# Hymba/MoE layer on one core: the last couple of experts gets a pass of its own order

## What is computed

```python
h = rms_norm(x, norm_ffn_g[l])
# top-1 group of 4, top-2 experts of its 8; combine[token, expert] holds the weights
a = jnp.einsum('sd,edf->sef', hs, w_gate)          # 32 experts, 1024 -> 256
u = jnp.einsum('sd,edf->sef', hs, w_up)
act = jax.nn.silu(a) * u * cs[..., None]
x = x + jnp.einsum('sef,efd->sd', act, w_down)     # 256 -> 1024
return rms_norm(x, norm_final_g)
```

## Time and profile before

| | us |
|---|---|
| median of 3 runs | 355.81 |
| the three runs | 355.76, 355.81, 357.69 |
| the profiled execution | 356.66 |
| its span | 354.8 |
| PE busy | 314.8 |
| DVE, ACT, POOL busy | 167.0, 121.1, 46.2 |
| mean DMA rate over the span | 341 GB/s |

### The profile page before, as it was taken

One profiled execution on the slowest core, in us unless ns is written; L12 is line 12 of the kernel. 1 busy time (PEld: TensorE's weight loads), 2 busy tenths in 40 slices (PEclk: granted clock), 3 DMA queues, 4 the chain that ended last, 5 costly groups with the idle time before them and its releaser, 6 DMA issues.

```text
span 354.8 us, 11527 instructions
## 1 busy us (share of the span) xinstructions
PE 314.8 (89%) x4766; PEld 244.4 (69%) x4767; DVE 167.0 (47%) x461; ACT 121.1 (34%) x308; POOL 46.2 (13%) x79
## 2 busy tenths in 40 slices
PE   8999999999999999979799899999999758649482
PEld 5999899799775446666577677777777555526460
DVE  4759285554164513844355355555555514322233
ACT  3544254463244237423233133333333302121113
POOL 3400001642504037600000000000000000000001
PEclk9999999999999999999999999999999989998878
DMA  7999994081849998699999999999999999999933
GB/s 270 321 388 386 386 396 171 14 342 21 336 136 388 307 400 328 235 294 411 421 404 385 413 421 409 417 421 414 422 417 414 413 413 426 414 416 420 415 127 118
DMA packets 33669, 121.07 MB, mean 341 GB/s; under 512 B 5624, under 2 KB 8080, under 8 KB 26480
## 3 DMA queue, kind: packets, MB, share of 16 engines
q1 hardware_dynamic: 33312, 120.63, 87.0%
q10 hardware_dynamic: 336, 0.14, 0.1%
HBM read 119.72 MB, written 1.05 MB: 340 GB/s over the span
## 4 chain that ended last, share of the span: by engine, by line
PE 69%; SPq 15%; DMA 6%; issue 3%; ACT 3%; DVE 2%; POOLq 0%; POOL 0%; ACTq 0%; DVEq 0%
PE bank L547 13%; PE bank L807 13%; SPq L389 8%; PE bank L614 7%; PE bank L839 6%; DMA spare<-in_w_up_dram 6%; PE bank L761 6%; PE bank L541 5%; SPq L401 5%; PE bank L768 3%; SPq L383 2%; PE bank L561 2%; PE bank L576 1%; PE bank L828 1%; PE bank L523 1%
## 5 line engine op out<-in xcount | busy, mean ns | idle before, releaser
L807 PE MATMUL bank<-ring,hT 128*32 128x128 f32 x1664 | 54.1, 283 | 18.7 <-DMA ring<-in_w_up_dram 8.7
L807 PEld LDWEIGHTS bank<-ring,hT 128*32 128x32 f32 x1664 | 47.7, 114 | 27.6 <-issue 27.4
L1546 DVE SCALAR_TENSOR_TENSOR yb<-bank,pp,yb 64x512 fp32r<-64x512 f32 x34 | 25.5, 750 | 50.8 <-ACT yb L1080 50.3
L1263 DVE TENSOR_TENSOR unit_lo<-ring,unit_hi 128x2048 fp32r<-128x2048 f32 (+1 forms) x12 | 26.5, 2209 | 28.7 <-ACT unit_hi L909 28.7
L1080 ACT ACTIVATE yb<-bank,pp 64x512 fp32r<-64x512 f32 x34 | 23.2, 683 | 35.4 <-PE bank L839 35.0
L761 PEld LDWEIGHTS bank<-pp,qk 128*128 128x128 bf16 x912 | 29.1, 100 | 8.1 <-issue 5.6
L761 PE MATMUL bank<-pp,qk 128*128 128x64 bf16 x912 | 31.4, 196 | 2.8 <-issue 2.8
L614 PE MATMUL bank<-ring,qk 128*128 128x512 f32 (+1 forms) x72 | 29.9, 551 | 0.0
L1225 POOL TENSOR_SCALAR stats<-qk 128x1 f32<-128x1 f32 x2 | 0.6, 311 | 200.5 <-ACT work L1100 200.5
L807 PE MATMUL bank<-work,hT 128*32 128x128 f32 x320 | 21.4, 288 | 5.4 <-DMA spare<-in_w_up_dram 2.9
L1529 DVE SCALAR_TENSOR_TENSOR pp<-bank,stats,pp 128x128 f32<-128x128 f32 x18 | 6.3, 351 | 41.5 <-ACT pp L1069 41.5
(11 more groups left out here) (217 smaller groups left out, 527.4 us busy)
## 6 DMA issues: line engine op xcount, KB each, us to landing
ring<-in_w_up_dram SPq DMA_DIRECT2D x24, 1024.0 KB, 16.7
ring<-in_w_down_dram SPq DMA_DIRECT2D x24, 1024.0 KB, 17.4
ring<-in_w_gate_dram SPq DMA_DIRECT2D x16, 1024.0 KB, 15.9
ring<-in_w_in_dram SPq DMA_DIRECT2D x5, 2048.0 KB, 19.7
ring<-in_w_gate_dram SPq DMA_DIRECT2D x16, 512.0 KB, 13.8
ring<-in_w_out_dram SPq DMA_DIRECT2D x4, 1024.0 KB, 12.8
spare<-in_w_gate_dram SPq DMA_DIRECT2D x4, 1024.0 KB, 18.7
spare<-in_w_up_dram SPq DMA_DIRECT2D x4, 1024.0 KB, 19.1
```

The lines of the kernel that those rows point to most:

```text
L807: last = mm(p_gu[b:b + CAP, w * P:(w + 1) * P], hg[:, k, CAP * e:CAP * (e + 1)], w_gu[at[e]][:, w, k, h, :], start=(k == 0), stop=(k == KD ...
L1263: V.tensor_tensor(unit_lo[b][:, k, :], unit_src(u)[:, k, :], unit_hi[b][:, k, :].bitcast(fp32), ALU.subtract).then_inc(w_lo_ready, 1)
L1546: V.scalar_tensor_tensor(out=yb[half][rest, :], in0=p_y[rows, :], scalar=wcol[rows, :], in1=yb[half][rows, :].bitcast(fp32), op0=ALU.mult, ...
```

## The change

- PE's loop runs 3 rounds instead of 4. The fourth round is written out behind it: `one_pass` for couples 12, 13 and 14 and a new `last_pass` for couple 15.
- `last_pass` has the same work in another order: the sums of the pass before first; four products that nobody reads; gates; picks; gather and the turned selection; three unread products; ups; three unread products; the activation turned round; then the downs in two halves, with the final norm's weights spread by two products of the PE ahead of each half.
- The downs of the places of couples 3, 7, 11 and 15 come in four transfers of 512 KB (first halves of both experts, then second halves), with a second semaphore. At the couples' first loading each expert's two halves are issued one after the other.
- The 512 KB transfer of the final norm's weights goes. One of 4 KB (`gfin4`, four rows) is issued ahead of the first refill. ACT and DVE copy the spread halves from the banks into `gfin`.

```diff
+            sp.dma_start(gfin4, I["norm_final_g"].rearrange("(r c) -> r c", r=4)).then_inc(gfin_in, 16)
             for q in range(TURN):
                 refill(q, [(2 * (q + TURN) + i, places(q)[i]) for i in range(2)])
             ...
-            sp.wait_ge(gate_done, sp.value_load(base[0:1, COUPLES - TURN + 1:COUPLES - TURN + 2], min_val=1, max_val=ITEMS_MAX))
-            sp.dma_start(gfin, I["norm_final_g"].rearrange("(o d) -> o d", o=1).to_broadcast([P, D])).then_inc(gfin_in, 16)
```

```diff
+            def load_dn_part(e, p, f):
+                src = I["w_down"][0, bass.ds(e, 1), f * P:(f + 1) * P].rearrange("o p n -> p (o n)")
+                sp.dma_start(w_dn[p][:, f], src).then_inc((dn_in, dn2_in)[f][p], 16)
...
-                for e, p in loads:
-                    load_dn(e, p)
+                if loads[0][1] in places(TURN - 1):
+                    for f in range(2):
+                        for e, p in loads:
+                            load_dn_part(e, p, f)
```

```diff
+            def last_pass(i, q, at, fillings, edge):
+                def unread_into(dst, n):
+                    for _ in range(n):
+                        mm(dst[:, :], identb, cb[:, 0:HALF], start=True, stop=True)
+                def spread_gfin(half, dst):
+                    for r in range(2):
+                        row = 2 * half + r
+                        mm(dst[:, r * SEQ:(r + 1) * SEQ], ident[0:4, row:row + 1].to_broadcast([4, P]), gfin4, start=True, stop=True)
+                pe.wait_ge(selT_ready, i + 1)
+                add_result(i)
+                unread_into(p_y, 4)
+                pe.wait_ge(hg_half_ready, i + 1)
...
+                    last = gate_or_up(0, k, at)
...
+                pe.wait_ge(sel_ready, i + 2)
+                gather(p_hg).then_inc(gathered, 1)
...
+                unread_into(p_y, 3)
+                for e in range(2):
+                    pe.wait_ge(up_in[at[e]], fillings * 16)
+                for k in range(KD):
+                    last = gate_or_up(1, k, at)
+                last.then_inc(gu_done, 1)
+                unread_into(p_y, 3)
+                pe.wait_ge(act_ready, i + 1)
+                nc.tensor.transpose(p_tr[:, 2 * P:3 * P], act_sb, ident).then_inc(actt_done, 1)
+                pe.wait_ge(gfin_in, 16)
+                spread_gfin(0, p_gu)
+                pe.wait_ge(actT_ready, i + 1)
+                for e in range(2):
+                    pe.wait_ge(dn_in[at[e]], fillings * 16)
+                downs(at, 0)
+                pe.wait_ge(hg_ready, i + 2)
+                spread_gfin(1, p_hg)
+                for e in range(2):
+                    pe.wait_ge(dn2_in[at[e]], fillings * 16)
+                downs(at, 1).then_inc(down_done, 1)
```

```diff
-            with pe.Fori(0, COUPLES // TURN) as g:
+            with pe.Fori(0, LOOPS) as g:
...
+            for j in range(TURN - 1):
+                with pe.Fori(passes_done, edge) as i:
+                    one_pass(i, LOOPS * TURN + j, places(j), LOOPS + 1, edge)
+                    pe.reg_add(passes_done, passes_done, 1)
+            with pe.Fori(passes_done, edge) as i:
+                last_pass(i, COUPLES - 1, places(TURN - 1), LOOPS + 1, edge)
+                pe.reg_add(passes_done, passes_done, 1)
```

```diff
             A(ylast[0:CP, :], p_y[0:CP, :], ACT.Copy, scale=wcol[0:CP, :]).then_inc(ylast_act, 1)
+            nc.scalar.copy(gfin[:, 0:HALF], p_gu[:, :]).then_inc(gfin_act, 1)
...
-            dve.wait_ge(gfin_in, 16)
+            V.tensor_copy(gfin[:, HALF:D], p_hg[:, :]).then_inc(gfin_dve, 1)
+            dve.wait_ge(gfin_act, 1)
+            dve.wait_ge(gfin_dve, 1)
```

More of the change, by code:

```diff
@@ L199, in layer_program @@
         gfin = ring[:, 0:D]
+        gfin4 = hT[:, :, :].rearrange("p a b -> p (a b)")[0:4, 3 * HALF + SEQ:3 * HALF + 2 * SEQ]
         rtr = qkf[:, D:2 * D]
@@ L281, in layer_program @@
         dn_in = [sem(f"dn_in{p}") for p in range(2 * TURN)]
+        dn2_in = {p: sem(f"dn2_in{p}") for p in places(TURN - 1)}
+        gfin_act, gfin_dve = sem("gfin_act"), sem("gfin_dve")
         out_done = sem("out_done")
@@ L398, in load_gu @@
                 load_half(e, p, 1)
+            def load_dn_part(e, p, f):
+                src = I["w_down"][0, bass.ds(e, 1), f * P:(f + 1) * P].rearrange("o p n -> p (o n)")
+                sp.dma_start(w_dn[p][:, f], src).then_inc((dn_in, dn2_in)[f][p], 16)
             def load_dn(e, p):
-                sp.dma_start(w_dn[p], I["w_down"][0, bass.ds(e, 1)].rearrange("o (h p) n -> p (o h) n", p=P)).then_inc(dn_in[p], 16)
+                if p in places(TURN - 1):
+                    load_dn_part(e, p, 0)
+                    load_dn_part(e, p, 1)
+                else:
+                    sp.dma_start(w_dn[p], I["w_down"][0, bass.ds(e, 1)].rearrange("o (h p) n -> p (o h) n", p=P)).then_inc(dn_in[p], 16)
             def load(e):
@@ L459, in refill @@
                 sp.wait_ge(down_done, passed)
-                for e, p in loads:
-                    load_dn(e, p)
+                if loads[0][1] in places(TURN - 1):
+                    for f in range(2):
+                        for e, p in loads:
+                            load_dn_part(e, p, f)
+                else:
+                    for e, p in loads:
+                        load_dn(e, p)
+            sp.dma_start(gfin4, I["norm_final_g"].rearrange("(r c) -> r c", r=4)).then_inc(gfin_in, 16)
             for q in range(TURN):
@@ L791, in add_result, with gate_or_up, downs @@
                 add_back(1).then_inc(added, 1)
+            def gate_or_up(w, k, at):
+                for h in range(2):
+                    for e in range(2):
+                        b = CP * h + CAP * e
+                        last = mm(p_gu[b:b + CAP, w * P:(w + 1) * P], hg[:, k, CAP * e:CAP * (e + 1)], w_gu[at[e]][:, w, k, h, :],
+                                  start=(k == 0), stop=(k == KD - 1))
+                return last
+            def downs(at, f):
+                for h in range(2):
+                    for e in range(2):
+                        b = CP * h + CAP * e
+                        last = mm(p_y[b:b + CAP, :], actT[:, CP * f + CAP * e:CP * f + CAP * (e + 1)],
+                                  w_dn[at[e]][:, f, h * HALF:(h + 1) * HALF], start=(f == 0), stop=(f == 1))
+                return last
             def one_pass(i, q, at, fillings, edge):
@@ L803, in one_pass @@
                             pe.wait_ge(hg_ready, i + 1)
[L804 to L808, removed]
+                        last = gate_or_up(w, k, at)
                         if w == 0 and k == KD // 2 - 1:
@@ L819, in one_pass @@
                 pe.wait_ge(base_ready, 1)
-                pe.reg_load(edge, base[0:1, bass.ds(q + 1, 1)])
+                pe.reg_load(edge, base[0:1, q + 1:q + 2] if isinstance(q, int) else base[0:1, bass.ds(q + 1, 1)])
                 pe.wait_ge(sel_ready, i + 2)
@@ L834, in one_pass @@
                     pe.wait_ge(dn_in[at[e]], fillings * 16)
[L835 to L841, removed]
+                    if at == places(TURN - 1):
+                        pe.wait_ge(dn2_in[at[e]], fillings * 16)
@@ new lines, in one_pass @@
+                downs(at, 0)
[13 more added lines that the diff above has]
+                for e in range(2):
+                    pe.wait_ge(gate_in[at[e]], fillings * 16)
+                for k in range(KD):
+                    if k == KD // 2:
+                        pe.wait_ge(hg_ready, i + 1)
+                    last = gate_or_up(0, k, at)
+                    if k == KD // 2 - 1:
+                        last.then_inc(gate_half_done, 1)
+                last.then_inc(gate_done, 1)
+                pe.wait_ge(selo_ready, i + 1)
+                for t in range(NT):
+                    picked = mm(p_tr[:, 3 * P + 1:3 * P + 4], selo[:, t, :], rst[:, t, :], start=(t == 0), stop=(t == NT - 1))
+                picked.then_inc(rr_done, 1)
+                pe.wait_ge(base_ready, 1)
+                pe.reg_load(edge, base[0:1, q + 1:q + 2])
+                pe.wait_ge(sel_ready, i + 2)
+                gather(p_hg).then_inc(gathered, 1)
+                pe.wait_ge(rrow_ready, i + 1)
+                pe.wait_ge(selw_ready, i + 1)
+                for t in range(NT):
+                    mm(p_tr[:, t * P:(t + 1) * P], selo[:, t, :], identb, start=True, stop=True)
+                for t in range(NT):
+                    mm(p_tr[:, 3 * P:3 * P + 1], selw[:, t, :], onescol, start=(t == 0), stop=(t == NT - 1))
+                unread_into(p_y, 3)
+                for e in range(2):
+                    pe.wait_ge(up_in[at[e]], fillings * 16)
+                for k in range(KD):
+                    last = gate_or_up(1, k, at)
[6 more added lines that the diff above has]
+                pe.wait_ge(actT_ready, i + 1)
+                for e in range(2):
+                    pe.wait_ge(dn_in[at[e]], fillings * 16)
+                downs(at, 0)
+                pe.wait_ge(hg_ready, i + 2)
+                spread_gfin(1, p_hg)
```

(3 more changed lines are left out.)

## The result

| | before | after |
|---|---|---|
| median, us | 356.06 (4 runs) | 362.17 (4 runs) |
| lowest to highest | 355.76 to 357.69 | 359.67 to 364.05 |
| profiled execution | 356.66 | 359.67 |
| its span | 354.8 | 357.9 |
| last ups landed | 335.0 | 338.3 |

The changed kernel is slower: ratio 1.0147, 95% interval 1.0100 to 1.0195. Two more medians of the same kernel, on other occasions, are 363.05 (4 runs, ratio 1.0181) and 362.69 (6 runs, ratio 1.0187). The kernel before was run again beside the later experiments, 29, 7, 29 and 23 times, and showed a much wider spread than its first runs: in the first 29 of these it reached from 353.25 to 359.55 with a median of 357.0. A ratio is taken between the runs that lie within 1.5% of the fastest of their own kernel, which leaves out up to seven of the slower runs of the kernel before, so it differs from the quotient of the medians by up to 0.6%.

The account below looks back on a forecast made before the run. Weights' landing bounds the kernel, so work behind the last ups counts. Last pass 0.15 plus clock fall 1.30 adds 1.45 us: 358.1 on the profiled execution, 357.3 as median (0.85 lower), range 354.0 to 359.4.

Parts of the forecast that it names:

- the last pass at full clock: Last pass in its new order, with no fall of the clock: ends 0.15 us later than in the kernel before.
- the spread: PE spreading the final norm's weights ahead of each downs half: 0.86 to 0.95 us first, 0.86 second, at full clock.
- The split downs: Last downs in four transfers: gains nothing; 4.4 us more of SP at most, covered by its 22 us lead.
- the 512 KB transfer: Final norm's weights, issued behind all other weights at 320.04 and wanted at 348.03: removing the transfer gains nothing.
- the two copies: ACT and DVE copying into gfin, behind ylast, 0.6 to 0.8 us each: cost nothing, with 0.5 us of cover on ACT.
- The ups of the last pass: Would start at 337.85, 2.8 us behind their landing at 335.0; still waiting for it would prove the prediction wrong.
- the end of yb: DVE's result of the pass before, ending at 331.46, for which the last pass's sums wait; start of the counted chain.
- rival 3: Instruction fetch stalls PE in the last pass's written-out code: 2.28 us gives 359.5, 0.98 gives 358.3; chance 0.10.
- its sign of being wrong: Last pass, from ups to downs: prediction wrong if this chain is longer than the 2.3 us counted.
- The 1.30 us: Clock falls to half behind 3 us of PE idling, slowing the last pass's gates or gather: 1.30 us added.
- rival 1: Clock holds in the last pass, all else as in the profile: 356.0 us; chance 0.24.
- Rival 4: SP or DMA becomes late, from small transfers or fetched code sharing the queues: 358 to 360 us; chance 0.06.

Follow-up runs that it names:

- e4: Kernel before with only the downs of couples 3, 7, 11 and 15 split into four transfers, old loop kept: 356.57 us, ratio 1.0018.
- f0: The changed kernel unchanged, run again for a second trace: 363.05 us, ratio 1.0181 to the kernel before.
- h1: The changed kernel unchanged, run once more on another chip: 362.69 us, ratio 1.0187 to the kernel before.
- h3: The changed kernel with spreading products over 128 array rows, 124 of them zeros, instead of four: 360.21 us, ratio 1.0118 to the kernel before.
- e2: Kernel before with the fourth round written out and the last pass's new order; no unread products, split or spread: 357.19 us, ratio 1.0021.
- e3: The changed kernel without its ten unread products: 363.24 us, ratio 1.0196 to the kernel before.
- h2: The changed kernel without the spread, final norm's weights by their 512 KB transfer, twelve runs: 358.21 us, ratio 1.0054 to the kernel before.
- f2: Kernel before with the fourth round written out and only the spread added, old order, downs whole: 360.82 us, ratio 1.0116.
- g4: The changed kernel with each spreading product issued twice into the same bank: 367.56 us, ratio 1.0315 to the kernel before.
- f4: The changed kernel with spreading products over 128 array rows, 124 of them zeros, first chip: 360.30 us, ratio 1.0125 to the kernel before.
- f1: The changed kernel without the spread, final norm's weights by their 512 KB transfer, first six runs: 359.89 us, ratio 1.0134 to the kernel before.
- e1: Kernel before with only the fourth round written out behind the loop, every pass in the old order: 357.43 us, ratio 1.0028.

## Why the prediction was wrong

**The forecast** was 357.3, range 354.0 to 359.4, with 0.85 on no change. The measured medians of 362.2 to 363.1 lie above the range. The direction (slower) was right, and so, to within 1 us, was the last pass at full clock; the step that failed was the spread, which was priced at full clock and at nothing behind it.

**What bounds it, and what is hidden.** Right as far as the runs tell. The split downs, the 512 KB transfer and the two copies were costed at nothing, and e4, with the split alone, is at 1.0018 (to 1.0060). In after, ACT's copy is done by 349.3, before line 1200 at 350.1, so the cover that was read from the earlier trace rows was there. The ups of the last pass no longer wait for their landing, as foreseen.

**The chain of the last pass, step by step.** It starts at the end of yb as said: 333.29 in after, 1.83 us later than the 331.46 of the earlier trace rows, because all of after is late. With that shift the sum had the ups end at 341.57; they ended at 342.08, of which 0.30 is a stall inside them (rival 3 at an eighth of its price). It had the downs start at 344.0; they started at 344.74: beside the 0.51 of the late ups the first spread took 1.05 instead of 0.86. From the ups to the downs are 2.66 us, 0.2 more than the sum had (339.74 to 342.2) and longer than the 2.3 that the prediction named as its sign of being wrong. The second spread was put at 0.86 and took 1.06, the halves of the downs at 0.95 and took 0.99 and 1.04. The end was foreseen at 346.8 and came at 347.83: 14.5 us instead of 13.5. One reading was off by little: line 807's first set in the earlier trace rows, the gates, takes 1.75, not the 1.88 used, but 1.88 is what the gates of after took.

**The clock ahead of the last pass.** The 1.30 us were not paid in the first trace of after, which is rival 1's case: clock 1.00 from 331 to 335, and 4.28 us from the first sum to the end of the gates (332.55 to 336.83). Where the clock fell there, it cost about the forecast's price: 5.87 in f0, 5.53 in h1 and 5.65 in h3, so 1.25 to 1.59 more, and 4.89 in e2 against 3.41 in e3, both without unread products. In f0 it is spread over sums, unread products and gates (2.16). The mechanism was right, and it is as open from run to run as rival 1 had it: of eleven traces with the sums first, four have the fall. So says the rule of the Trainium skill that the prediction cited (TensorE: Matmul & The Clock Gate, Part 1), and three traces of one and the same kernel agree: the stretches of low clock begin at 170.8, 171.1 and 172.3 us and in the last pass nowhere (after), at 334.9 (f0) and at 332.7 (h1).

**The step that failed: the spread as a sum of instructions.** The prediction priced the two spreads by their columns at full clock, 0.86 each, with 0.23 of the first and all of the second counted as added (342.2 against 341.97, then 0.86), 1.09 together. Its only term for the clock, 1.30, stands ahead of the gates and asks whether PE had been idle; behind the spread it has none. The spread itself took more: from the turned activation's start to the end of the downs are 2.65 us in h2 (without it), 4.29 in h3 (full rows) and 4.47 in after, so 1.6 to 1.8. And in five of six traces with four-row products the clock was low in or behind them, and in four of these (e3, f0, f2, g4) it stayed so through all of the last sums. The same sums in before, on the chain of the earlier trace rows:

```profile
345.94 2.00 PE bank L775 x8
```

In e3, f0, f2 and g4 they (line 792) take 3.80. On one chip, in ratios to before: 1.0187 with four rows (h1), 1.0118 with full rows (h3), 1.0054 without (h2). So of 1.9% some 0.7% (2.5 us) is the clock behind the four rows, some 0.6% (2.3 us) the spread's own time and waits, and 0.5% the rest. The intervals of neighbours overlap (1.0133 to 1.0241, 1.0063 to 1.0172, 1.0016 to 1.0092), so these parts are rough. The means of all runs give the same picture on both chips: 362.69, 360.30 and 358.06 on this one, 363.12 (f0), 360.13 (f4) and 358.75 (f1) on the other, so 2.4 and 3.0 us for the four rows, 2.2 and 1.4 for the spread.

**What stays open.** The rest of 0.5% (order, unread products, split and written-out code together) is larger than written-out code alone (0.28%), with the order (0.21%), with order and unread products (0.36%) or the split alone (0.18%). All these intervals overlap, so no run tells if the parts add up or act together, or if the rest is there at all in this size.

**The base of the forecast.** The three runs shown had a median of 355.81; 29 runs have 357.0 and reach from 353.25 to 359.55. That spread has a place, at least in part: the stall of the earlier trace rows at 169 us, which no code of the change touches. It is there in all 18 traces, 2.2 to 2.8 us long. All but three (before, e3, f1) have a low clock behind it, for about 3.4 or 6.8 us. In these fifteen the DMA share of 186 to 188 us is 0.19 to 0.57, in the three 0.80 to 0.90; and the three have the earliest landings, 335.0 to 335.5, against 335.9 to 338.6. The prediction read the stall as a matter of fetched code only, and not that a clock could fall behind it and pass the loss on through SP to the last landing. **Rival 3** in its own form did not happen at its price: stalls in the ups of the last pass are 0.30 (after) and 0.84 us (e3, 337.70). **Rival 4** fell with e4.

The Trainium skill (Runtime: NRT & Kernel Launch, Instruction fetch mechanics) has straight code fetched ahead and mostly hidden. For the written-out round the runs agree (e1, 1.0028). The stalls of 0.30 and 0.84 stand in straight code, behind product 41 of the ups in after and behind product 48 in e3, which lacks the seven unread products ahead of them: the same place in the row of PE's instructions. That fits a fetch that came late, but no run tests it.

## What to carry to other kernels

A product that is put on the PE to save a transfer can cost more than its columns: look at how many rows of the array it uses and at what stands behind it, and price the work behind it at half clock as well. Part a trace at the last landing of weights: what lies before it and what behind it vary for reasons of their own, and a single profiled span mixes the two (here the first trace showed 3.1 us of the first, and nothing of the 4 to 6 us of the second that the next two traces of the same kernel had). When work is moved ahead of a wait, put first what needs only what has landed, and last what another engine is still making; here the tail went from 18.6 to 19.8 us in the old order to 16.3 to 17.6, though the timed runs (0.9991 to 1.0019) don't yet show a gain from it.

## What the runs showed of the hardware

- The granted clock fell in or just behind products that used four rows (4x128 weights, 256 columns of fp32, eight instructions of 374 ns each in 2.1 us), in the middle of PE's busy time in f0, f2 and g4. With the same products over 128 rows, 124 of them zeros, in nearly the same time (0.87 to 1.06 us for four instructions), no fall came in two traces, and the kernel was 2.5 to 2.8 us faster.
- Once at 0.50 it stayed there in f0 from 348.6 on, through the rest of the spread, 1.91 us of downs (128x32 weights) and 3.80 us of sums (64x128 weights), with one gap of 1.1 us between, though PE was busy in single microseconds to 1.00.
- A low clock of 3.4 to 6.8 us at 170 us went with a landing 165 us later that came 0.4 to 3.6 us later than in the three traces without it, and with DMA queues that ran dry for 2 to 4 us in between (share 0.19 to 0.57 at 186 to 188 us against 0.80 to 0.90).
